# One input column more ahead of the recurrence's first drive, and the second read-out half a column sooner

## What is computed

```python
h = rms_norm(x, pre_g)
proj = jnp.einsum("bld,de->ble", h, w_in)
conv_in, z_c, u_s, z_s, g_c, g_s = jnp.split(proj, IN_OFFSETS, axis=-1)
ca, cb = jnp.split(conv_in, 2, axis=-1)
cu = silu(layer_norm(causal_depthwise_conv(ca * sigmoid(cb), conv_w, conv_b), ...))
conv_out = (cu * silu(z_c)) @ w_conv_out
y = gelu(s5_mimo(u_s, ...))          # a complex state-space recurrence over the tokens
...
return x + rms_norm(merged @ w_out, post_g)
```

## Time and profile before

| | |
|---|---|
| median of 3 runs | 2077.75 us (2074.13 to 2077.99) |
| the profiled execution's own time | 2078.3 us |
| its span in the trace | 2076.2 us |
| PE busy | 2027.2 us, 98% of the span |
| DVE, ACT, POOL busy | 1373.2, 638.2, 242.8 us |
| mean granted clock of PE | 0.994 |
| zc columns and recurrence | 1204.9 to 1357.3 us of the span |

### The profile page before, as it was taken

How to read it: one execution, slowest core, us unless ns; L and a number is a source line. 1 busy time by engine, 2 the same in 40 slices (tenths; PEclk the granted TensorE clock), 3 DMA queues, 4 the chain that set the end, 5 groups by cost and what they waited for, 6 DMA issues and landing times. The chain is left out here.

```text
span 2076.2 us, 21462 instructions
## 1 busy us (share of the span) xinstructions
PE 2027.2 (98%) x7218; PEld 1100.8 (53%) x7218; DVE 1373.2 (66%) x1920; ACT 638.2 (31%) x1065; POOL 242.8 (12%) x188
## 2 busy tenths in 40 slices
PE   7999999999999999999998999999999999999998
PEld 4444444448678668767454455544444444444443
DVE  3787785366666676676525695449999996435633
ACT  4345443334435344334125220014211112341021
POOL 0000001123213213311004000011000000004200
PEclk9999999999999999999998999999999999999999
DMA  9333379521111111112311244399412221333021
GB/s 351 127 116 97 114 266 245 137 69 44 38 37 50 40 35 44 38 48 75 88 34 57 106 74 82 100 266 248 106 56 71 72 74 58 116 101 132 21 105 57
DMA packets 243825, 207.17 MB, mean 100 GB/s; under 512 B 52205, under 2 KB 202786, under 8 KB 243746
## 3 DMA queue, kind: packets, MB, share of 16 engines
q1 hardware_dynamic: 213393, 157.25, 25.5%
q0 software_dynamic: 13056, 42.99, 8.3%
q10 hardware_dynamic: 17312, 6.10, 1.4%
HBM read 182.55 MB, written 60.33 MB: 117 GB/s over the span
## 5 line engine op out<-in xcount | busy, mean ns | idle before, releaser
L2490 PE MATMUL bank<-hT,ring 128*128 128x512 f32 x576 | 254.2, 592 | 0.0
L2490 PE MATMUL bank<-resid,ring 128*128 128x512 f32 x432 | 191.3, 592 | 0.0
L2490 PEld LDWEIGHTS bank<-hT,ring 128*128 128x128 f32 x576 | 109.4, 190 | 137.8 <-issue 136.6
L1441 PE MATMUL bank<-hT,ring 128*128 128x512 f32 (+1 forms) x448 | 163.8, 488 | 1.8 <-ACT silu_z L1680 1.8
L3410 DVE SCALAR_TENSOR_TENSOR yT<-s_arena,yT 128x1024 f32<-128x1024 f32 x120 | 152.9, 1274 | 0.0
L3410 DVE SCALAR_TENSOR_TENSOR s_arena<-s_arena 128x1024 f32<-128x1024 f32 x112 | 142.7, 1274 | 0.0
L2462 PE MATMUL bank<-hT,ring 128*128 128x512 f32 x320 | 139.4, 594 | 0.0
L2490 PEld LDWEIGHTS bank<-resid,ring 128*128 128x128 f32 x432 | 82.1, 190 | 103.3 <-issue 102.6
L2462 PEld LDWEIGHTS bank<-hT,ring 128*128 128x128 f32 x320 | 60.1, 190 | 73.7 <-issue 73.5
L1441 PEld LDWEIGHTS bank<-hT,ring 128*128 128x128 f32 x448 | 77.5, 191 | 33.5 <-issue 29.4
L1441 PE MATMUL bank<-resid,yT 128*128 128x256 f32 (+1 forms) x280 | 85.1, 422 | 0.0
(11 more groups left out here) (603 smaller groups left out, 3660.7 us busy)
## 6 DMA issues: line engine op xcount, KB each, us to landing
ada<-in_ada_w SPq DMA_DIRECT2D x8, 2048.0 KB, 8.1
ring<-in_gdn_in_w SPq DMA_DIRECT2D x32, 512.0 KB, 4.1
ring<-in_w_in SPq DMA_DIRECT2D x54, 256.0 KB, 2.9
ab_U_sums<-in_w_in POOLq DMA_DIRECT2D x6, 2048.0 KB, 18.8
resid<-in_x SPq DMA_DIRECT2D x8, 1024.0 KB, 8.9
ring<-in_lru_in_w SPq DMA_DIRECT2D x16, 512.0 KB, 3.9
ring<-ab_U_sums SPq DMA_DIRECT2D x32, 256.0 KB, 2.9
lru_arena<-in_ada_w SPq DMA_DIRECT2D x6, 1024.0 KB, 13.3
```

Source lines behind the costliest of these rows:

```text
L1441: last = nc.tensor.matmul(bank[:, to, cols_], w[:, k, :], v[:, k, cols_], start=(first and k == 0 and n == 0), stop=(k == KB - 1), skip_gr ...
L2490: last = nc.tensor.matmul(bank[:, to, :], w[:, k, :], src[:, k, :], start=(start and k == 0), stop=(k == HK - 1), skip_group_check=not alone)
```

## The change

zc3 is moved ahead of `drive(0)`, and each later zc column moves up in the same way. Between `drive(0)` and `read_out(0)` there are still one and a half columns, but now zc4 and the first half of zc5. Between `drive(1)` and `read_out(1)` there were two columns (zc5, zc6), and now there are one and a half: zc6 and the first half of zc7. The second half of zc7 comes behind `read_out(1)`. ACT takes zc4 ahead of `y0`, and SP loads zc6 ahead of `store_y(0)`. No instruction is added or taken away.

```diff
 # pe_b, the order of PE's steps
-"zc1", "zc2", "w0", "zc3", "y0", "zc4", "w1", "zc5", "zc6", "y1", "zc7"
+"zc1", "zc2", "zc3", "w0", "zc4", "y0", "zc5", "w1", "zc6", "y1", "zc7"
 # act_b
-"zc1", "zc2", "zc3", "y0", "zc4", "zc5", "zc6", "y1", "zc7"
+"zc1", "zc2", "zc3", "zc4", "y0", "zc5", "zc6", "y1", "zc7"
 # sync
                     load("zc5", w_in, ZC + 5)
+                    load("zc6", w_in, ZC + 6)
                     store_y(0)
-                    load("zc6", w_in, ZC + 6)
 # tensor
                     finish(early("zc2"))
+                    finish(early("zc3"))
                     act_b.wait(pe, "B1")
                     pe.wait_ge(u_loaded, BLK // 2 * 16)
                     pe.wait_ge(u_loaded_act, BLK // 2 * 16)
                     drive(0)
-                    finish(early("zc3"))
-                    tile = early("zc4")
+                    finish(early("zc4"))
+                    tile = early("zc5")
                     next(tile)
                     dve_b.wait(pe, "s0")
                     pe.wait_ge(K_placed, BLK * 16)
                     read_out(0)
                     finish(tile)
                     act_b.wait(pe, "y0")
                     drive(1)
-                    finish(early("zc5"))
                     finish(early("zc6"))
+                    tile = early("zc7")
+                    next(tile)
                     dve_b.wait(pe, "s1")
                     read_out(1)
-                    finish(early("zc7"))
+                    finish(tile)
 # scalar
+                    silu_c(4)
                     take_y(0)
-                    silu_c(4)
```

More of the change, by code:

```diff
@@ L2253, in block_program @@
             pe_b = Steps(sem("second_pe"), [x for t in range(11) for x in ([f"final{t}"] if t < TT else []) + ([f"flip{t - 3}"] if t >= 3 else [])
-                                            + (["u0_first"] if t == 8 else ["u1_first"] if t == 9 else [])] + ["u0", "c_flip", "u1", "u2", "u3", "kernel0", "kernel1", "zc0", "B_flip0", "B_flip1", "zc1", "zc2", "w0", "zc3",
-                                            "y0", "zc4", "w1", "zc5", "zc6", "y1", "zc7"]
+                                            + (["u0_first"] if t == 8 else ["u1_first"] if t == 9 else [])] + ["u0", "c_flip", "u1", "u2", "u3", "kernel0", "kernel1", "zc0", "B_flip0", "B_flip1", "zc1", "zc2", "zc3", "w0", "zc4",
+                                            "y0", "zc5", "w1", "zc6", "y1", "zc7"]
                          + [x for name in PAIR_ORDER[:14] for x in [f"{name}_{q}" for q in PRODUCTS] + (["sums"] if name == "gs3" else []) + SINGLE_AFTER.get(name, [])]
@@ L2261, in block_program @@
                           + ["root_x", "dt", "mag", "rho", "sin", "cos_abs", "cos", "u0", "u1", "u2", "u3", "kernel0", "kernel1", "zc0", "B0", "B1",
-                                              "zc1", "zc2", "zc3", "y0", "zc4", "zc5", "zc6", "y1", "zc7"]
+                                              "zc1", "zc2", "zc3", "zc4", "y0", "zc5", "zc6", "y1", "zc7"]
                           + ["ab0_kept0", "ab0_kept2", "ab0_kept1", "ab0_kept3", "ab0_sig2", "ab0_sig21"] + acts("ab1")
```

## The result

The changed kernel takes 2079.43 us, median of 20 runs, against 2076.66 us for the kernel before, also 20 runs: a ratio of 1.0014, 95% interval 1.0008 to 1.0021. One run of each took far longer (5533.37 and 3592.96 us) and is left out of the ratio; over the other 19 the medians are 2079.31 and 2076.00 us. The change is about 2.8 us slower, between 1.7 and 4.4. That is inside the 0.2% that the prediction counted as no change, but the interval lies wholly above 1. The profiled execution took 2078.15 us, span 2076.1; that it lies level with the profiled execution of before (2078.3) is chance, as will be seen.

A forecast was written before the change was run, and what follows sets the result against it. PE was taken as the bound, busy 2027.2 of 2076.2 us. Wait +1.8, clock -0.8 and P7's block +0.5 gave +1.5 us on a median of 2077.75: 2079.3 us, range 2074.5 to 2082.5.

The forecast's parts named there:

- the range of the sum: Whole change, all terms at their bounds together: between -0.6 and +3.6 us.
- The rule of the sum: Around the zc columns: every us PE wins or loses there reaches the end, and nothing else can give more.
- 6.8 us: First drive in the kernel before: 4.39 us of wait plus 2.41 of slow clock, all the change has to win.
- PE stops at the same place for another load: After zc2: zc3's weights land at 1259.72, so PE waits for them, 6.2 us instead of 4.39.
- Rival A: Before zc3: its weights land before 1253.64, all 6.8 us won, 0.5 paid back at P7; 2071.5 us, chance 0.10.
- Wait +1.8: After zc2: PE's wait, now for zc3's weights, is 6.2 us instead of 4.39, a cost of 1.8 us.
- clock -0.8: Start of zc3: half clock loses 1.6 us where the drive lost 2.41, -0.8 us, bounds -2.4 to 0.
- It fell before the drive had begun, so it falls again: Wait after zc2: PE's clock falls as before, returns at 1263.00, and 3.2 us of zc3 run at half clock.
- P7's block, 0.5 us between 0 and 1.75: Fifth product of ab0: its block, queued behind the load of y, makes PE wait 0.5 us, bounds 0 to 1.75.
- The chain to the load of y: Behind the second read-out: 11.39 us from its end, through `y1` and 16 stores, to the issue of y's load.
- Second read-out: After the second drive: one and a half columns cover DVE's 19.2 us with 1.5 to spare; no wait, no gain.
- Rival B: Fifth product of ab0: P7's block takes over 12 us to land, PE waits long, slower by over 0.2%; chance 0.08.

The follow-up runs named there:

- both moves: Changed kernel with zc3's load issued ahead of the u loads, and P7's and P3's blocks ahead of the second stores and load of y: 2071.07 us, ratio 0.9980.
- half a column more of lateness: Changed kernel with the whole of zc7 ahead of the second read-out in PE's order: 2088.13 us (4 runs), ratio 1.0057 to the kernel before.
- the new issue order: Kernel before, PE's order kept, with SP's load of zc3's weights issued ahead of the four u loads: 2080.35 us, ratio 1.0019.

## Why the prediction was right, and what was off

**The number is closer than the working.** Forecast were 2079.3 us, measured 2079.43, and that is luck. The forecast set +1.5 us on a median of three runs, 2077.75; over 20 runs the kernel before has 2076.66, and the change costs 2.8. An error of 1.1 in the one and 1.3 in the other cancel. What stands is the class (no difference clear of 0.2%), the direction, and the range of the sum, -0.6 to +3.6.

**The rule of the sum held.** PE was the bound, and beyond its wait at the first drive and P7's block nothing gave or took anything. In all ten profiles the waits from 1420 on are the old ones. But 6.8 us was not what there was to win: with both waits gone the kernel is 5.3 us quicker by the medians and 4.2 by the ratio.

**"PE stops at the same place for another load" was the step that mattered, and it is shown.** The load took 17.7 us and ended the wait. The experiment that moved only that load took 7.5 us off the changed kernel (expected 6.8); the two medians are from two measurements, between which the kernel before moved by 0.2. Rival A, by which the weights lie ready and all is won, was a right price (2071.5 us) for a case that the order of SP's list excludes; that experiment, at 2071.93, is rival A made true.

**Wait +1.8 and clock -0.8.** For the two profiled executions the sum of both terms was forecast at +1.0 and came out at +0.1 (103.73 against 103.64 us). In the second, zc3's load was issued 0.7 us earlier against zc2's end and landed 0.9 us quicker, so the wait grew by 0.2 only instead of 1.8. The clock lost 2.1 instead of 1.6 us: the slow stretch ended 8.9 us after zc2, near the 9.4 of the forecast, but zc3 had begun 1.6 us sooner than forecast, so 4.30 us of it ran at 1.2 GHz and not 3.2.

For the medians the error goes the other way. The term that was off most is the base: I took 6.8 us as what the first drive costs in the kernel before, from one execution. In two other profiles of that order the wait was 2.75 and 3.31 us and the clock did not fall, so it cost only that. The mean over three is 4.3 us. In the changed order the mean over four is 4.6 of wait and 1.3 of clock, 5.9. The difference, 1.6 us instead of 1.0, and 1.0 for P7 make 2.6, near the 2.8 measured. This is an estimate from three and four executions, some of them of edited kernels with the same order at the first drive. The medians of the experiments price the two stops independently of it: 5.3 us for the old one (both moves against the kernel before) and 7.5 for the new one (zc3's load moved, against the changed kernel), which puts the difference at about 2. Both prices lie above the means of the profiles (4.3 and 5.9), and why is open.

Either way the clock term of -0.8 has the wrong sign as a likely value: in these profiles the slow clock cost 0.8 us on average in the old order and 1.3 in the new one. "It fell before the drive had begun, so it falls again" was the step behind it, and it does not follow: in one of four profiles of the new order the clock did not fall. That the change moves a wait which often escapes the slow clock to one that seldom does fits the record (mean granted clock of 0.997 or more in 20 of 46 runs of the kernel before, in 2 of 19 of the changed one), but that clock also holds the stretch from 1100 to 1150, so it is not shown.

**P7's block, 0.5 us between 0 and 1.75.** It was 1.03 us in the first profile (product's start), 1.43 in the second (1355.44 to 1370.60). Both pieces of the estimate were off, against each other. The chain to the load of y was longer than 11.39 us: the 16 stores took 8.66 us to issue instead of 7.48, and the load of y followed their last issue by 2.14 us instead of 1.89. In the changed kernel ACT's store of zc7 goes out among them. In the seven profiles in which a zc store does, they took 8.6 to 9.0 us, in the other three 7.5; that the one causes the other was not tested alone. In return the block needed 8.4 us, less than the 9.3 (10.6 less 1.3) that I had said. That the block waits behind y, and that the lateness of y decides, is shown from both sides: with the block issued ahead of y the wait is gone, with half a column more of lateness it grows by 7.0 us.

**Second read-out.** The forecast of 1.5 us to spare and no wait is right in the trace. DVE ends at 1337.42 (the last instruction below) and the read-out starts at 1338.87:

```profile
1336.20 1.22 DVE L3349 TENSOR_TENSOR s_arena<-yT 128x1024 f32<-128x1024 f32 x1
```

**Rival B** did not come about: P7's block landed in 8.4 and 8.8 us and not over 12. But its mechanism is real. One half column further it costs 8 us and the clock with it, though by y's lateness and not by a slower block (8.7 us).

## What to carry to other kernels

When work is moved forward to fill a wait, ask when its own operands land. A load that was never waited for is not therefore early; here it was issued right behind the very loads that caused the wait. Move the load together with the work that needs it: alone the new order lost 2.8 us and the new issue order 3.9, together they won 4.5, each against the kernel before of its own measurement. And a stop that the slow clock sometimes lengthens can't be priced from one profile: here one execution said 6.8 us and the medians 5.3. Behind each step that is moved later against the bound engine, follow the queue to the first small load that stands behind a large one.

## What was not expected of the hardware

A wait of PE in this place cost more than its length only in some executions. At the first drive or zc3, waits of 2.75, 3.31 and 3.63 us left the granted clock at 2.4 GHz, waits of 4.39, 4.58, 4.89, 5.36 and 6.91 us had it at 1.2 GHz for a while, which lost another 1.5 to 2.4 us. These are eight executions; where between them the limit lies, if there is one, was not measured. And the time to landing had little to do with size: 256 KB took 16.5 us and 512 KB 17.7 while the DMA engines were full (share 1.2), and 512 KB 4.1 us in the median.
